# Attention steps of a streaming-encoder layer taken in twos on TensorE: transposes of a chunk's two groups together, global heads in pairs

## The reference

```python
x = x + 0.5 * swiglu(rms_norm(x, ffn1_norm), ffn1_w1, ffn1_w3, ffn1_w2)
h = rms_norm(x, mix_norm)
c_q, c_kv, k_pe, q_s, k_s, v_s = jnp.split(h @ w_in, IN_SPLIT_POINTS, axis=-1)
y_mla = mla_attention(c_q, c_kv, k_pe, ...) @ w_o_mla     # 8 heads, block-causal over all 512 keys, blocks of 128
y_swa = swa_attention(q_s, k_s, v_s, rel_bias, sinks) @ w_o_swa   # 16 heads, 2 key heads, chunks of 64, band of 128 keys
g_mla, g_swa = jnp.split(jax.nn.sigmoid(h @ w_gate), 2, axis=-1)
x = x + (g_mla * y_mla + g_swa * y_swa) @ w_out
x = x + 0.5 * swiglu(rms_norm(x, ffn2_norm), ffn2_w1, ffn2_w3, ffn2_w2)
return rms_norm(x, final_norm)
```

## Time and profile before

| | us |
|---|---|
| median of 3 runs | 1117.87 (1117.73 to 1118.08) |
| the profiled execution | 1117.91 |
| its span, first to last instruction | 1116.1 |
| PE busy | 1105.7 |
| DVE busy | 561.2 |
| ACT busy | 415.2 |
| POOL busy | 144.0 |
| the attentions, from 426 to 636 us: PE busy | 207.9 of 210 |

### The profile page before, as it was taken

The page is one execution under the profiler, slowest core; times in us unless marked ns, Lnnn a source line. Parts: engine busy times, 40 slices in busy tenths (PEclk is TensorE's granted clock), DMA queues, the critical chain, the costliest instruction groups (busy, mean ns, idle before and its releaser), DMA issues.

```text
span 1116.1 us, 14662 instructions
## 1 busy us (share of the span) xinstructions
PE 1105.7 (99%) x5166; PEld 898.8 (81%) x5166; DVE 561.2 (50%) x846; ACT 415.2 (37%) x715; POOL 144.0 (13%) x112
## 2 busy tenths in 40 slices
PE   9999999999999999999999999999999999999997
PEld 7888888888888887677777788888888888888896
DVE  6644344433446436865666554546443344434453
ACT  7322222222235324676645533344221223212243
POOL 0211011100114102321000002231110011100111
PEclk9999999999999999999999999999999999999999
DMA  7235222332224321232312222222233322322222
GB/s 270 88 98 123 96 95 94 94 100 101 101 70 119 112 95 58 61 91 85 114 57 77 75 96 94 95 94 95 95 94 100 106 96 94 95 94 95 85 85 76
DMA packets 34893, 107.73 MB, mean 97 GB/s; under 512 B 4240, under 2 KB 6960, under 8 KB 34848
## 3 DMA queue, kind: packets, MB, share of 16 engines
q1 hardware_dynamic: 34224, 105.82, 29.2%
q0 software_dynamic: 192, 0.78, 0.7%
q10 hardware_dynamic: 432, 0.54, 0.1%
HBM read 102.29 MB, written 2.88 MB: 94 GB/s over the span
## 4 chain that ended last, share of the span: by engine, by line
PE 96%; DVE 2%; ACT 1%; issue 1%; POOL 0%; DMA 0%; SPq 0%; POOLq 0%; DVEq 0%; ACTq 0%
PE bank L1411 29%; PE bank L1413 28%; PE bank L1412 28%; PE bank L1565 2%; PE bank L1592 1%; PE bank L1616 1%; PE bank L1551 1%; PE bank L1602 1%; PE bank L1756 1%; PE bank L1758 1%; PE bank L1757 1%; PE bank L1776 0%; PE bank L1774 0%; PE bank L1775 0%; PE bank L1523 0%
## 5 line engine op out<-in xcount | busy, mean ns | idle before, releaser
L636 ACT ACTIVATE w_hi<-staged 128x1024 fp32r<-128x1024 f32 x182 | 193.1, 1061 | 547.9 <-PE bank L1413 547.9
L1411 PE MATMUL bank<-xg_hi,w_hi 128*128 128x512 f32 x1000 | 394.8, 395 | 0.0
L1413 PE MATMUL bank<-xg_hi,w_lo 128*128 128x512 f32 x1000 | 389.5, 390 | 0.0
L1412 PE MATMUL bank<-xg_lo,w_hi 128*128 128x512 f32 x1000 | 389.3, 389 | 0.0
L956 DVE TENSOR_TENSOR w_lo<-staged,w_hi 128x1024 fp32r<-128x1024 f32 x182 | 223.8, 1229 | 112.7 <-ACT w_hi L636 112.7
L1411 PEld LDWEIGHTS bank<-xg_hi,w_hi 128*128 128x128 f32 x1000 | 187.7, 188 | 44.6 <-issue 6.2
L1413 PEld LDWEIGHTS bank<-xg_hi,w_lo 128*128 128x128 f32 x1000 | 187.7, 188 | 39.9
L1412 PEld LDWEIGHTS bank<-xg_lo,w_hi 128*128 128x128 f32 x1000 | 187.8, 188 | 38.9 <-issue 1.2
L535 POOL TENSOR_TENSOR h_lo<-hid,h_hi 128x512 f32 x44 | 70.7, 1607 | 590.6 <-ACT h_hi L659 534.8
L1411 PE MATMUL bank<-h_hi,w_hi 128*128 128x512 f32 x304 | 118.4, 389 | 0.2 <-POOL h_lo L535 0.2
L1413 PE MATMUL bank<-h_hi,w_lo 128*128 128x512 f32 x304 | 118.3, 389 | 0.0
(11 more groups left out here) (203 smaller groups left out, 1012.4 us busy)
## 6 DMA issues: line engine op xcount, KB each, us to landing
staged<-in_ffn_w SPq DMA_DIRECT2D x118, 512.0 KB, 3.3
staged<-in_w_gate SPq DMA_DIRECT2D x16, 512.0 KB, 3.5
staged<-in_w_in SPq DMA_DIRECT2D x15, 512.0 KB, 3.3
staged<-in_ffn_w SPq DMA_DIRECT2D x16, 384.0 KB, 3.1
staged<-in_w_ob SPq DMA_DIRECT2D x8, 512.0 KB, 3.3
staged<-in_w_out SPq DMA_DIRECT2D x8, 512.0 KB, 3.3
x<-in_x_t SPq DMA_DIRECT2D x8, 256.0 KB, 4.8
staged<-in_w_oa SPq DMA_DIRECT2D x4, 512.0 KB, 3.3
```

The costliest lines, as they stand in the source:

```text
L636: nc.scalar.activation(w_hi[:, u % SPLIT, :], staged[:, u % STAGED, :], ACT.Copy).then_inc(hi_done, 1)
L1411: nc.tensor.matmul(o, wh, hi, start=start, stop=False)
L1412: nc.tensor.matmul(o, wh, lo, start=False, stop=False)
L1413: return nc.tensor.matmul(o, wl, hi, start=False, stop=stop)
```

## The change

In `fillers()`, Newton's step moves from slot 5 to slot 6, the first unit product of the keys (`uk`, 0) from slot 9 to slot 8, `uk` 2 from slot 10 to 9, `uk` 3 from slot 11 to 10, and the explicit split of the first `uq` unit goes, so that this unit is split by the general rule. PE's loop now takes two steps at a time from step 2 on: both transposes, then the scores of the next chunk (or of two global steps), the values of the chunk or pair before, then the pieces of two slots. In the global half the scores of both steps stand ahead of both transposes. ACT copies both transposes of a chunk, then splits, reads the output, and does the exponentials of the even step, and those of the odd step behind the even slot's pieces. DVE does `scores(n+2)`, the split for slot n, `scores(n+3)`, the pieces of slot n+1, `normalise(n+2)`, the split for slot n+1, `normalise(n+3)`, the pieces of slot n+2. Inside the first `scores(1)`, `normalise(0)` stands behind the maximum.

```diff
-            [("newton", 0, "kv"), ("gate", 0, 0)],
-            [("scale", 0, "kv"), ("gate", 0, 1), ("round", 0, "kv"), ("latent", 4, 0)],
+            [("gate", 0, 0)],
+            [("newton", 0, "kv"), ("scale", 0, "kv"), ("gate", 0, 1), ("round", 0, "kv"), ("latent", 4, 0)],
             [("rest", 0, "kv"), ("latent", 4, 1)],
-            halves("gate", 1),
-            [("uk", 0, 0), ("uk", 1, 0)],
-            [("sum", 0, "q"), ("rest", 3, "q"), ("rest", 4, "q"), ("uk", 2, 0), ("gate", 2, 0)],
-            [("split", 0, "uq"), ("uk", 3, 0), ("gate", 2, 1)],
+            halves("gate", 1) + [("uk", 0, 0)],
+            [("uk", 1, 0), ("uk", 2, 0)],
+            [("sum", 0, "q"), ("rest", 3, "q"), ("rest", 4, "q"), ("uk", 3, 0), ("gate", 2, 0)],
+            [("gate", 2, 1)],
...
@@ ACT @@
-            for n in range(STEPS):
-                if n % 2 == 1 and n + 2 < W_STEPS:
+            for n in range(W_STEPS):
+                if n == 1:
                     exponentials(n + 2)
-                read_transposed(n)
+                if n < 2:
+                    read_transposed(n)
+                elif n % 2 == 0:
+                    read_transposed(n)
+                    read_transposed(n + 1)
+                else:
+                    exponentials(n + 2)
                 split_next(PLAN[n])
...
@@ DVE @@
+            normalise(1)
+            for n in range(0, W_STEPS, 2):
+                scores(n + 2)
+                split_next(PLAN[n])
+                scores(n + 3)
+                for piece in PLAN[n + 1]:
+                    filler(*piece)
+                normalise(n + 2)
+                split_next(PLAN[n + 1])
+                normalise(n + 3)
+                for piece in PLAN[n + 2]:
+                    filler(*piece)
...
@@ PE @@
+            for c in range(1, NC):
+                transposes(2 * c)
+                transposes(2 * c + 1)
+                if c + 1 < NC:
+                    band_scores(c + 1)
+                else:
+                    scores(W_STEPS)
+                    scores(W_STEPS + 1)
+                swa_values(c - 1)
+                for piece in PLAN[2 * c + 1] + PLAN[2 * c + 2]:
+                    filler(*piece)
+            for n in range(W_STEPS, STEPS, 2):
+                if n + 2 < STEPS:
                     scores(n + 2)
+                    scores(n + 3)
                 transposes(n)
-                if n + 2 < W_STEPS and n % 2 == 0:
-                    band_scores(n // 2 + 1)
-                if 2 <= n <= W_STEPS and n % 2 == 0:
-                    swa_values(n // 2 - 1)
-                elif n > W_STEPS and n % 2 == 0:
+                transposes(n + 1)
+                if n == W_STEPS:
+                    swa_values(NC - 1)
+                else:
                     mla_values(n - 2)
-                for piece in PLAN[n + 1]:
+                for piece in PLAN[n + 1] + PLAN[n + 2]:
                     filler(*piece)
```

More of the change, by code:

```diff
@@ L860, in _ @@
             exponentials(1)
-            for n in range(STEPS):
-                if n % 2 == 1 and n + 2 < W_STEPS:
+            for n in range(W_STEPS):
+                if n == 1:
                     exponentials(n + 2)
-                read_transposed(n)
+                if n < 2:
[5 more added lines that the diff above has]
+                    exponentials(n + 2)
                 split_next(PLAN[n])
-                if n >= 1:
-                    read_output(n - 1)
-                if (n % 2 == 0 or n + 2 >= W_STEPS) and n + 2 < STEPS:
+                if n % 2 == 0:
+                    if n:
+                        read_output(n - 1)
                     exponentials(n + 2)
@@ L874, in _ @@
                     if piece[0] != "latent":
+                        filler(*piece)
+            for n in range(W_STEPS, STEPS, 2):
+                for step in (n, n + 1):
+                    if step + 2 < STEPS:
+                        exponentials(step + 2)
+                    read_transposed(step)
+                for step in (n, n + 1):
+                    split_next(PLAN[step])
+                    read_output(step - 1)
+                    for piece in PLAN[step + 1]:
                         filler(*piece)
@@ L1150, in scores @@
                     done(nc.vector.tensor_reduce(smax[:, n % 2, :], tiles, AX.X, ALU.max, negate=True))
+                    if n == 1:
+                        normalise(0)
                     done(nc.vector.tensor_tensor(nmax[:, n % 2, :], smax[:, n % 2, :], sink_neg[:, kv, :], ALU.min))
@@ L1295, in _ @@
             scores(1)
-            normalise(0)
             for piece in PLAN[0]:
                 filler(*piece)
-            for n in range(STEPS):
-                if n + 1 < STEPS:
-                    normalise(n + 1)
-                if n + 2 < W_STEPS:
-                    if n % 2 == 0:
-                        scores(n + 2)
-                    split_next(PLAN[n])
-                    if n % 2 == 0:
-                        scores(n + 3)
-                elif n + 2 < STEPS:
+            normalise(1)
[10 more added lines that the diff above has]
+                    filler(*piece)
+            for n in range(W_STEPS, STEPS, 2):
+                if n + 2 < STEPS:
                     scores(n + 2)
-                    split_next(PLAN[n])
-                else:
-                    split_next(PLAN[n])
+                    scores(n + 3)
+                split_next(PLAN[n])
                 for piece in PLAN[n + 1]:
+                    filler(*piece)
+                if n + 2 < STEPS:
+                    normalise(n + 2)
+                    normalise(n + 3)
+                split_next(PLAN[n + 1])
+                for piece in PLAN[n + 2]:
                     filler(*piece)
@@ L1697, in _ @@
                 filler(*piece)
-            for n in range(STEPS):
-                if W_STEPS <= n + 2 < STEPS:
+            for n in range(2):
+                transposes(n)
+                if n == 0:
+                    band_scores(1)
+                for piece in PLAN[n + 1]:
+                    filler(*piece)
+            for c in range(1, NC):
[8 more added lines that the diff above has]
+                for piece in PLAN[2 * c + 1] + PLAN[2 * c + 2]:
+                    filler(*piece)
+            for n in range(W_STEPS, STEPS, 2):
+                if n + 2 < STEPS:
                     scores(n + 2)
+                    scores(n + 3)
                 transposes(n)
-                if n + 2 < W_STEPS and n % 2 == 0:
-                    band_scores(n // 2 + 1)
-                if 2 <= n <= W_STEPS and n % 2 == 0:
-                    swa_values(n // 2 - 1)
-                elif n > W_STEPS and n % 2 == 0:
+                transposes(n + 1)
+                if n == W_STEPS:
+                    swa_values(NC - 1)
+                else:
                     mla_values(n - 2)
-                for piece in PLAN[n + 1]:
+                for piece in PLAN[n + 1] + PLAN[n + 2]:
                     filler(*piece)
```

## The result

The change makes the kernel slower: 1130.32 us in the median of 4 executions (1129.86 to 1131.73) against 1117.97 for the kernel before on the same chip, a ratio of 1.011 with a 95% interval of 1.0098 to 1.0122, or +12.3 us. The direction was forecast, the size was not: the forecast was +5.1 us, with a range that ended at 1126.5. The profiled execution took 1130.40 us, span 1128.6.

What follows compares the result with a forecast made beforehand. TensorE (PE), busy 1105.7 of 1116.1 us, was taken to bound the kernel, so only its work or stand-stills count. Waits of 7.7 us after against 2.6 before gave +5.1 on 1117.9, hence 1123.0 us, range 1119.0 to 1126.5.

Steps and rivals of the forecast that it cites:

- PE's own work in pairs: Joining two steps on PE costs and saves nothing: a chunk's fp32 block stays at 3.2 us.
- T(0): Step 0's transposes: normalise(0) starts about 0.3 us sooner, so 0.2 us of the 0.46 us wait is left.
- T(3): Step 3's transposes, the first that were a slot later: wait of 1.7 us (0.9 to 2.2).
- T(5): Step 5's transposes, after 24 matmuls and two small products: wait of 0.9 us (0 to 1.3).
- Unit of gate 1: Chunk 3's block: Newton's operations, now behind den(7), make this unit late; PE waits 1.6 us (0.8 to 2.2).
- T(7): Step 7's transposes: 36 matmuls and no split before den, so no wait, 0.
- T(13): Step 13's transposes: 30 matmuls in slots 11 and 12 are too few; wait of 2.1 us (1.5 to 2.6), the surest term.
- Second half: Global heads in pairs: short chain, a low part ahead of two scores around step 20; wait of 0.2 us (0 to 2).
- Part 2: Each chunk's second group of transposes loses a slot; its chain takes 10.4 us from the block's start, before queue delays.
- the waits only move: Rival, no change, chance 0.17: about 4.2 us of waits against 2.6, 1119.5 us.
- the pairs are covered: Rival, faster, chance 0.06: the windowed half's chain fits under two slots, only 0.2 us of waits left, 1115.5 us.
- The second half waits too: Rival, slower, chance 0.10: eight of the sixteen global pairs wait 0.4 us each, adding 3.2 us, 1126.2 us.

Runs made afterwards that it cites:

- run 5: The changed kernel with den and rden of step 13 on DVE ahead of the low part of slot 11's unit: 1129.74 us.
- run 4: The kernel before with the new table of slots and the earlier normalise(0), but its own loops: 1115.74 us, ratio 0.9977.
- run 7: The changed kernel with two more places for the copied transposes, PE's order untouched: 1123.89 us, ratio 1.0050 to the kernel before.
- run 9: The kernel of run 7 with Newton's step back in slot 5: 1122.95 us, ratio 1.0038 to the kernel before.
- Run 10: The kernel of run 9 with step 13's den and rden, and both normalises in the global pairs, ahead of the low parts on DVE: 1120.40 us.
- three stall runs: The kernel of run 4 with three, three and a half or four needless POOL additions ahead of step 14's multiplication: 1118.14, 1120.13 and 1121.84 us.
- run 8: The changed kernel with each windowed block on PE ordered scores, values, transposes: 1124.81 us, ratio 1.0060 to the kernel before.
- run 12: The kernel of run 4 with slot 10's third key product put behind the half of gate 2: 1118.35 us.

## Why the prediction was wrong

The sign was right, the size wrong: +12.3 against +5.1. Step by step, waits as idle time unless "by starts" is said:

- **What bounds the kernel, and PE's own work in pairs (0):** right. A chunk's joined block takes 3.18 us where nothing waits (run 5, steps 10 and 11), and the two blocks of run 4 take 2.74 + 0.44 = 3.18.
- **T(0), 0.2:** right (starts 0.20 late). What I added, that POOL's multiplication would hold up the two small operations, did not come: both had started before it (432.12 and 432.29 against 432.36) and took 0.13 and 0.16 us.
- **T(3), 1.7:** 1.5 by PE's starts (1.31 idle). Right.
- **T(5), 0.9:** T(5) 0.76, but T(4) ahead of it waits 0.85 too: 2.0 by starts. Run 7 takes T(4)'s away and halves T(5)'s.
- **Unit of gate 1, 1.6:** 1.54 by starts, and run 9 shows the cause. Right.
- **T(9), 1.0:** 0.6 by starts. **T(7), 0:** 1.1 by starts (0.90 idle).
- **T(13), 2.1:** 2.14 (2.31 by starts), and 1.7 on top that I had nowhere. So close a hit has luck in it: 0.5 of it came from ACT's late queue, since in run 7 the wait is 1.60.
- **Key unit, query unit and slot 10, 0:** 0.5 by starts, 0.7 (0.5 before), and 0.9 more than before. Slot 10 and the query unit are ACT's queue, late by the values: in run 7 neither waits. The key unit waits there as it did (0.35), and no longer in run 9: that is Newton's place again. I had no term for slot 10's 0.6 of before, and no reason for its going, and had not named the 0.2 at the query unit.
- **Second half, 0.2:** 1.7 by starts, near the upper end of my bounds; the four pairs with 512 keys have 0.3 to 0.4 each. I named the right place ("around step 20 the low part stands ahead of two scores") and the rival its right size (0.4 at each), but for four pairs, not eight.

Two slips of arithmetic changed nothing: the high ends add up to +9.4, not +9.5, and by Part 2's own numbers 30 fillers (10.5 us) just cover the 10.4, while the text puts them with those that do not. Run 10 agrees with the numbers: with nothing ahead of den, T(13) waits nowhere behind 30.

Two steps failed, and one term was mis-sized. The first step is the chain of Part 2 with the terms built on it: I let ACT copy the transposes as soon as they are there (0.60 us each) and did not ask what else the copy waits for. Its rows before would have told: in the earlier trace rows the copy L771 is released by L1602, the values. They then stood right behind one group's transposes and the scores, now behind one group more. By run 7 against the change this is 4.4 us of waits.

The second is the price of a wait. I counted each at its length. Behind T(13)'s 2.1 us the clock was lost as well, another 1.7 us in the trace. The mis-sized term is that of the second half, 1.7 against 0.2.

Without the first two, run 7 measured 1123.89 where the prediction said 1123.0. That they are so close is luck in part. By starts, T(3), T(5), gate 1's unit, T(9) and T(13) wait 1.5, 0.5, 1.5, 0.6 and 1.8 us in it, 1.4 less than I had put down for the five, and T(7), the key unit and the second half make up for it, which I had at 0, 0 and 0.2.

The rivals: *the waits only move* and *the pairs are covered* fell. *The second half waits too* came true in a part, as an addition to mine.

Beside the second step stands one sentence of the Trainium skill, TensorE: Matmul & The Clock Gate, Terms: the penalty of a throttled time is about that time multiplied by one less the granted share. The rows agree: 1.7 us by the clock column, and 0.81 + 0.81 us of longer scores and values at T(13), which have most of that time. On the rule weighed in the prediction (SBUF — State Buffer, Who interferes with whom), the trace has a row of its own now. Newton's second operation, with both inputs in SBUF, started beside POOL's multiplication and took 1.41 us instead of the 0.69 of before (first row); the multiplication, which had started beside Newton's first operation, was stretched too, 1.33 instead of 1.04:

```profile
465.58 0.69 DVE L1211 TENSOR_TENSOR root_sq<-root_sq,lat_half 128x512 f32<-128x512 f32 x1
```

```profile
471.27 0.66 DVE L1227 TENSOR_TENSOR root_sq<-acc 128x512 f32<-128x512 f32 x1
...
471.50 1.33 POOL L576 TENSOR_TENSOR probs<-probs,rden 128x512 f32<-128x512 f32 x1 [0.72 <-DVE rden L1192]
...
471.97 1.41 DVE L1229 TENSOR_TENSOR root_sq<-root_sq,lat_half 128x512 f32<-128x512 f32 x1
```

By that rule the multiplication does hold up DVE, and here it did. It did so at another place than the two that I had assumed, and the 0.3 us by which it was stretched itself are a part of T(7)'s wait, since this is N(7).

**Left open.** In four executions the clock's part of the change can't be averaged well: the profiled one lost it once, at T(13), and mean clocks of 0.996 in others hint at more. Whether the 0.6 us of run 4 can be had in another order was tried twice and not found. A version in twos that beats run 4 was not found; since joined blocks cost PE exactly what single ones do, it could win about that 0.6 at most.

## What to carry to other kernels

- Before moving a step, list everything that its consumer waits for, buffers that come free included. A copy that waits for "the data there" and for "the place free" follows the later of the two, and on an engine with one queue all behind it follows too. The row of the copy names which one it is.
- Price a stand-still of TensorE by more than its length: here one of about 2 us cost 1.7 us more in some executions, one of 3.3 us at least that in all. In the trace of run 7, whose longest waits are 1.3, 1.3 and 1.6 us, nothing was lost.
- Changes that come in one diff need not belong together: the table of slots with the earlier normalise(0) was worth -2.3 us by itself, and the windowed loops in twos that it came with cost 15.

## What was not expected of the hardware

The clock's fall costs the same each time that a trace shows it (1.7 us by the clock column at T(13), behind slot 10, and in all three stall runs), and it comes by chance: behind a wait of 1.9 us the same program took about 1118.0 or 1119.4 us. The shortest wait with a fall behind it in a trace is that of 1.2 us at slot 10 in run 8, where the clock had fallen once 15 us before; the longest without one is that of 1.9 us in run 12. A timing of few executions then reads as noise what is a second, real price. The kernel before has none of it in the attention (longest wait 1.0 us).
